# Two ranked experts of a pair, gate and up: unit by unit in turn instead of one expert after the other, with a fourth pair of half buffers

## The reference

```
vals, idx = lax.top_k(t @ router, 2)
gates     = softmax(vals)
combine   = sum(one_hot(idx, 8) * gates[..., None], 1)
for e in range(8):
    out = out + combine[:, e:e+1] * (silu(t @ wg[e]) * (t @ wu[e])) @ wd[e]
```

## Time and profile before

| | us |
|---|---|
| median of three runs | 1655.17 (1654.16 to 1659.08) |
| the profiled execution, its own time | 1653.77 |
| its span in the profile | 1652.0 |
| TensorE busy | 1599.2 (97%) |
| VectorE busy | 1216.1 (74%) |
| ScalarE busy | 980.4 (59%) |
| experts, first to last product | about 1228 to 1634 |

### The profile page before, as it was taken

One profiled execution on the slowest core, in us unless ns is written; L12 is line 12 of the kernel. 1 busy time (PEld: TensorE's weight loads), 2 busy tenths in 40 slices (PEclk: granted clock), 3 DMA queues, 4 the chain that ended last, 5 costly groups with the idle time before them and its releaser, 6 DMA issues.

```text
span 1652.0 us, 27749 instructions
## 1 busy us (share of the span) xinstructions
PE 1599.2 (97%) x10996; PEld 1449.5 (88%) x10996; DVE 1216.1 (74%) x1751; ACT 980.4 (59%) x1419; POOL 309.1 (19%) x307
## 2 busy tenths in 40 slices
PE   8999999999999999999999999999999999999997
PEld 7988888898888889998999999999997878777786
DVE  5555786666668666998875554799987887888887
ACT  6556665346657634555554443555558867777775
POOL 1331552123217501143120002132120000000000
PEclk9999999999999999999999999999999999999999
DMA  8632555555335555543435455543519999999982
GB/s 295 239 106 101 177 181 203 180 197 186 106 135 194 179 204 179 175 148 117 165 120 189 176 179 179 170 154 128 178 73 387 328 366 327 365 330 335 364 333 78
DMA packets 50774, 339.76 MB, mean 206 GB/s; under 512 B 5639, under 2 KB 7903, under 8 KB 11439
## 3 DMA queue, kind: packets, MB, share of 16 engines
q1 hardware_dynamic: 47920, 328.79, 55.9%
q0 software_dynamic: 2720, 9.13, 1.8%
HBM read 336.76 MB, written 1.13 MB: 205 GB/s over the span
## 4 chain that ended last, share of the span: by engine, by line
PE 81%; ACT 7%; DVE 6%; issue 3%; POOL 1%; DMA 0%; DVEq 0%; ACTq 0%; SPq 0%; POOLq 0%
PE bank L578 12%; PE bank L552 8%; PE bank L554 8%; PE bank L553 8%; PE bank L576 7%; ACT wh L1342 5%; PE bank L997 3%; PE bank L709 3%; PE bank L999 3%; DVE wl L1911 3%; PE bank L998 3%; PE bank L711 3%; PE bank L710 3%; PE bank L1005 1%; PE bank L1006 1%
## 5 line engine op out<-in xcount | busy, mean ns | idle before, releaser
L1911 DVE TENSOR_TENSOR wl<-stg,wh 128x2048 fp32r<-128x2048 f32 x266 | 610.8, 2304 | 209.6 <-ACT wh L1342 209.2
L1342 ACT ACTIVATE wh<-stg 128x2048 fp32r<-128x2048 f32 x266 | 507.1, 1910 | 131.0 <-PE bank L999 44.3
L552 PE MATMUL bank<-xx,wh 128*128 128x272 f32 (+1 forms) x778 | 225.5, 290 | 0.0
L554 PE MATMUL bank<-xx,wl 128*128 128x272 f32 (+1 forms) x778 | 223.3, 287 | 0.0
L553 PE MATMUL bank<-xx,wh 128*128 128x272 f32 (+1 forms) x778 | 223.1, 287 | 0.0
L578 PE MATMUL bank<-xx,wh 128*128 128x512 f32 x448 | 159.7, 396 | 0.0
L578 PE MATMUL bank<-H,wh 128*128 128x512 f32 x434 | 151.3, 390 | 0.0
L553 PEld LDWEIGHTS bank<-xx,wh 128*128 128x128 f32 x778 | 147.5, 190 | 0.0
L552 PEld LDWEIGHTS bank<-xx,wh 128*128 128x128 f32 x778 | 146.3, 188 | 1.1 <-issue 0.7
L554 PEld LDWEIGHTS bank<-xx,wl 128*128 128x128 f32 x778 | 146.3, 188 | 0.0
L709 PE MATMUL bank<-wh,xx 128*128 128x256 f32 x480 | 139.7, 291 | 0.8 <-DVE zm L1985 0.8
(11 more groups left out here) (432 smaller groups left out, 3810.7 us busy)
## 6 DMA issues: line engine op xcount, KB each, us to landing
stg<-in_w SPq DMA_DIRECT2D x178, 1024.0 KB, 5.0
stg<-in_units SPq DMA_DIRECT2D x86, 1024.0 KB, 6.9
sq<-in_units SPq DMA_DIRECT2D x22, 1024.0 KB, 6.8
stg_more<-in_units SPq DMA_DIRECT2D x20, 1024.0 KB, 6.9
BT<-bias_scratch POOLq DMA_DIRECT2D x3, 1024.0 KB, 10.5
BT<-bias_scratch POOLq DMA_DIRECT2D x1, 2048.0 KB, 12.9
BB<-bias_scratch POOLq DMA_DIRECT2D x2, 1024.0 KB, 6.5
stg<-in_tails SPq DMA_DIRECT2D x4, 512.0 KB, 4.9
```

The costliest lines, as they stand in the source:

```text
L552: pe.matmul(out, wh, xh(kt), start=kt == 0, stop=False)
L554: ins = pe.matmul(out, wl, xh(kt), start=False, stop=kt == KT - 1)
L1342: act.activation(WH[u % NW][:, :], stg[stage_of(u)][:, :], ACT.Copy).then_inc(*m.inc("w_high", u))
L1911: vec.tensor_tensor(WL[u % NW][:, :], stg[stage_of(u)][:, :], WH[u % NW][:, :].bitcast(F32), ALU.subtract).then_inc(*m.inc("w_low_v", u))
```

## The change

It takes the gate and up products of a pair's two experts unit by unit in turn, and the units are loaded in that order (`PAIR_UNITS`, `phases`): in a group first all gate rows (a unit of the big expert, one of the small, a unit of the big, one of the small), then all up rows likewise. Only the very first group (pair 0, group 0) keeps the old order. `turn` of a group moves behind the first three big gate rows of the next group, for the last group behind the first two rows of the down products; `turn_and_sum` stands three small rows further on. There is a fourth pair of half buffers (`wh_more`, `wl_more`): ScalarE may round unit u when unit u-4 is finished. Room comes from the second `G` and from one staging buffer (five instead of six). With one `G`, the gathering of the next pair's tokens stands inside the down products. The arm for the case that an expert has more than 128 tokens is changed in the same way and does not run with these inputs.

```
-MORE = 2
+MORE = 1
...
-PAIR_UNITS = [(s, 4 * gi + n) for gi in range(2) for s in range(2) for n in range(4)] + [(s, 8 + n) for s in range(2) for n in range(3)] \
-    + [(s, 11 + n) for n in range(5) for s in range(2)] + [None]
+LATER_UNITS = [(s, n) for n in range(16) for s in range(2)] + [None]
+PAIR_UNITS = [[(s, n) for s in range(2) for n in range(4)] + LATER_UNITS[8:]] + [LATER_UNITS] * 3
...
+def ring_of(u):
+    if u < RING_FROM:
+        return u % NW
+    k = (u - RING_FROM) % (NW + 1)
+    return NW if k == 0 else (RING_FROM + k - 1) % NW
+
+def last_in_ring(u):
+    return u - NW if u < RING_FROM else u - NW - 1
...
+def phases(j, gi):
+    n0, nn = GU[gi]
+    every = [(s, up, kt) for s in range(2) for up in range(2) for kt in range(KD)]
+    if j == 0 and gi == 0:
+        return [every[KD * i:KD * (i + 1)] for i in range(4)]
+    by_unit = lambda r: ((2 * KD * n0 + (r[1] * KD + r[2]) * nn) // UT, r[0], r[2])
+    return [sorted([r for r in every if r[1] == up], key=by_unit) for up in range(2)]
...
-            stg += [flat(SQ)[:, 0:UT * P], sb("stg_more", [P, UT * P], F32, st)[:, :]]
+            stg += [flat(SQ)[:, 0:UT * P]]
+            WH += [sb("wh_more", [P, UT * P], F32R, st)]
+            WL += [sb("wl_more", [P, UT * P], F32R, st)]
...
-                G = [sb(f"G{i}", [P, KD, 3 * P], F32R, sp) for i in range(2)]
+                G = sb("G", [P, KD, 3 * P], F32R, sp)
...
                     for gi in range(3):
...
+                        for i, phase in enumerate(phases(j, gi)):
+                            for s, up, kt in phase:
+                                one_row(s, gi, up, kt)
+                                if gi > 0 and (s, up, kt) == (0, 0, 2):
+                                    turn("sp", big, gi - 1, 0, mtm2[0])
+                                if gi > 0 and (s, up, kt) == (1, 0, 2):
+                                    turn_and_sum(few_, gi - 1)
+                            if gi == 0 and i == 0:
+                                if j == 0:
+                                    gather_small()
+                                else:
+                                    scatter(j - 1, (2, 3))
+                            if gi == 1 and i == 0:
+                                select(big)
+                                select(few_)
...
                     def hook(n, s, i_step):
                         if (n, s, i_step) == (0, 0, 1):
+                            turn("sp", big, 2, 0, mtm2[0])
+                        if (n, s, i_step) == (0, 1, 1):
                             turn_and_sum(few_, 2)
+                        if 0 < n < 5 and (s, i_step) == (0, 3) and j < PAIRS - 1:
+                            gather(j + 1, n - 1)
...
 class Splits
             def enter(self, u):
-                while self.made < min(u + NW, N_UNITS) and not self.held:
+                while self.made < N_UNITS and last_in_ring(self.made) < u and not self.held:
                     self.split(self.made)
                     self.made += 1
...
 ScalarE, split
-                    w.wait_ge(*m.of("group" if u - NW < EXPERT_UNIT else arm[0], ("unit", u - NW)))
-                act.activation(WH[u % NW][:, :], stg[stage_of(u)][:, :], ACT.Copy).then_inc(*m.inc("w_high", u))
+                    w.wait_ge(*m.of("group" if last_in_ring(u) < EXPERT_UNIT else arm[0], ("unit", last_in_ring(u))))
+                act.activation(WH[ring_of(u)][:, :], stg[stage_of(u)][:, :], ACT.Copy).then_inc(*m.inc("w_high", u))
...
 VectorE, sparse
+                        for i, phase in enumerate(phases(j, gi)):
+                            for s, up, kt in phase:
+                                sp.row(j, gi, s, up, kt)
+                                if gi > 0 and (s, up, kt) == (1, 0, 0):
+                                    low(big, gi - 1)
+                                if gi > 0 and (s, up, kt) == (0, 0, 6):
+                                    small_hidden(few_, gi - 1)
+                                if gi > 0 and (s, up, kt) == (1, 0, 7):
+                                    small_low(few_, gi - 1)
+                            if (0, 1, KD - 1) in phase:
+                                hidden_of("sp", big, gi, 0, mtmp[0], mtm2[0], last)
+                            if gi == 0 and i == 0:
+                                if j < PAIRS - 1:
+                                    choose(2 * j + 2)
+                                    choose(2 * j + 3)
+                                if j > 0:
+                                    scatter(j - 1, (2, 3))
```

More of the change, by code:

```diff
@@ L1007, in in_two @@
                 return product
[L1009 to L1032, removed]
@@ L1034, in turn, with row @@
-            def turn(tag, x, gi, i, j):
+            def row(tag, j, s, gi, up, kt, products, read, operand):
+                x, (n0, nn) = 2 * j + s, GU[gi]
+                first = 2 * KD * n0 + (up * KD + kt) * nn
+                if kt == 0:
+                    for i in range(len(products)):
+                        b, old = bank((tag, "gu", x, gi, up, i), (read, (x, gi, i)))
+                        held.add(b)
+                        vacant(old)
+                operand(kt)
+                pieces = [(unit_of(j, s, n), k, c, o) for n, k, c, o in pieces_of(first, nn)]
+                for i, product in enumerate(products):
+                    b = m.bank[tag, "gu", x, gi, up, i]
+                    for pi, (u, k, c, o) in enumerate(pieces):
+                        if k == 0:
+                            unit_ready(u)
+                        ins = product(PS[b][:, o * P:(o + c) * P], kt, WH[ring_of(u)][:, k * P:(k + c) * P], WL[ring_of(u)][:, k * P:(k + c) * P])
+                        over = i == len(products) - 1 and k + c == UT
+                        if kt == KD - 1 and pi == len(pieces) - 1:
+                            ins.then_inc(*m.inc(f"group_{tag}", ("gu", x, gi, up, i)))
+                            if over:
+                                m.also(f"group_{tag}", ("unit", u))
+                            let_go(b)
+                        elif over:
+                            ins.then_inc(*m.inc(f"group_{tag}", ("unit", u)))
+                at[0] += nn
@@ L1036, in turn @@
+            def turn(tag, x, gi, i, hidden):
                 nn = GU[gi][1]
@@ L1161, in nothing @@
                         pass
-                    for gi in range(3):
[L1164 to L1185, removed]
@@ L1206, in hidden_product, with turn_all @@
                     return in_three(lambda kt: EHH[s][:, kt, i * P:(i + 1) * P], lambda kt: EHL[s][:, kt, i * P:(i + 1) * P], 10)
[L1208 to L1212, removed]
+                def turn_all(j, gi):
+                    for s in range(2):
                         for i in range(2):
-                            turn("et", x, gi, i, i)
+                            turn("et", 2 * j + s, gi, i, mtm4[2 * s + i])
                 for j in range(PAIRS):
                     for gi in range(3):
[L1218 to L1223, removed]
+                        for i, phase in enumerate(phases(j, gi)):
+                            for s, up, kt in phase:
+                                row("et", j, s, gi, up, kt, [product(0), product(1)], "hidden_et" if up else "gate_et", operand)
+                            if gi > 0 and i == 0:
+                                turn_all(j, gi - 1)
+                    turn_all(j, 2)
                     down("et", j, [[hidden_product(s, i) for i in range(2)] for s in range(2)], lambda x, g, i: [("summed", (x, g, i))],
@@ L1313, in take, with row @@
                 self.at += n
+            def row(self, j, gi, s, up, kt):
+                n0, nn = GU[gi]
+                self.low = max(self.low, unit_of(j, 0, 0))
+                for n, k, c, o in pieces_of(2 * KD * n0 + (up * KD + kt) * nn, nn):
+                    u = unit_of(j, s, n)
+                    self.used[u] = self.used.get(u, 0) + c
+                while self.used.get(self.low) == UT:
+                    self.low += 1
+                self.at += nn
+                self.enter(self.low)
             def run(self, n):
```

229 lines of the change are left out of this document (110 added, 119 removed).

## The result

The changed kernel takes 1697.29 us in the median of four runs (1696.83 to 1699.4), the one before 1655.41 (four runs): a ratio of 1.0252 (95% interval 1.0233 to 1.0270). It is slower by 42 us, where 38 were forecast, and 1697 lies in the range. (A slip ahead of the prediction: the first piece of TensorE's order shown there reads G1, which is the buffer of the second and the fourth pair, so it isn't of the third.)

The account below looks back on a forecast made before the run. TensorE was taken to bound the kernel, a pair being its work plus stalls. Net stalls of +23.3 us and a slower clock of +15.2 made +38.5 on the profiled 1653.8, said as 1693 for the median; range 1670 to 1710.

Parts of the forecast that it names:

- What bounds the stage: Expert stage: a pair's 100.4 us are TensorE's work plus stalls, some 6.5 us of them; weights wait for VectorE.
- the third rival: Weight loading: with five staging buffers instead of six the weights become the bound, 1709 us; chance 0.07.
- The new stalls: At `turn`: it waits for hidden values that stand behind four splits, 48.4 us in 11 stalls.
- What it removes: In the expert stage: 16.8 us of stalls at `turn` and 9.1 us of other stalls go.
- A pair: Expert stage of the changed kernel: a pair takes 108 to 111 us instead of 100.4.
- The clock: TensorE behind the 11 new stalls: one slow stretch of 1.6 us each, less 2.4 for those of now, +15.2 us.
- The first rival: TensorE: the stalls come as worked out but the clock stays as it is, +23.3 us, 1678; chance 0.27.
- the second rival: End of a group: hidden values come in time; `turn` at E + 4.4 breaks even, at E + 2 gives 1629; chance 0.05.

Follow-up runs that it names:

- e7: The changed kernel with big hidden values ahead of both last splits, group 2's small ones ahead of a split, and later transposes at the down products: 1625.65 us, ratio 0.9816.
- e1: The changed kernel with the big expert's hidden values moved on VectorE ahead of both of the group's last splits: 1632.49 us, ratio 0.9842.
- e5: The changed kernel with the transposes of big hidden values moved from behind the third to behind the sixth big gate row of the next group: 1675.06 us, ratio 1.0101.
- e8: The changed kernel with the big expert's hidden values on VectorE between the group's last two splits: 1657.12 us, ratio 1.0013.
- e6: The changed kernel with matmuls of constants (7 and 11) ahead of the 11 late transposes, filling most of each stall: 1678.09 us, ratio 1.0141.
- e3: The changed kernel with the units and rows of gate and up in the old order again, all else as changed: 1633.63 us, ratio 0.9838.
- e4: The kernel before, with the big expert's hidden values on VectorE ahead of the split that its last up row releases: 1648.36 us, ratio 0.9954.

## Why the prediction was right, point by point

**What bounds the stage.** Right: a pair is TensorE's work plus stalls. e7 without stalls runs at 93 us for a pair (92.9 to 93.3 from one start of the down products to the next), and 100.4 less 6.5, 93.9, was said. The transfers, at 345 GB/s before, carry 374 there: they were not the bound, and the third rival is out (ScalarE waited 4 us for them in the whole stage of the changed kernel). They are near it in e7, busy 97% in the window above, and ScalarE waits 6.9 us for them.

**The new stalls.** 48.4 us forecast, 48.1 measured, in 11 cases as said, and shown by e1, e5 and e8 from both sides. The sum is better than its terms, and in that it was lucky (second pair, E is the end of the group):

| | `turn` starts, forecast | measured | stall, forecast | measured |
|---|---|---|---|---|
| group 0 | E + 6.5 (5.7 in the last pair) | E + 5.5 | 4.4 (3.6) | 3.4 |
| group 1 | E + 5.7 | E + 5.6 | 4.1 | 4.0 |
| group 2 | E + 6.3 | E + 7.9 | 4.9 | 5.5, and 0.9 ahead of the down products |

In group 0 I had VectorE too late. It was through with the choice of tokens and the additions when the up phase's first unit was ready:

```profile
1354.67 1.28 DVE L2604 TENSOR_TENSOR res<-res,bank 128x512 f32<-128x512 f32 x2
1355.86 6.82 DVE L1957 TENSOR_TENSOR wl<-stg,wh 128x2048 fp32r<-128x2048 f32 x3
```

So it began the four splits some 5.1 us into the phase, where 5.0 was reckoned for group 1. The last pair, which chooses nothing, has the same stall of 3.4. In group 2 I had it too early. The step that failed is the start of its four splits at 3.7 us into the phase; they began at 5.8. ScalarE stood still just before; the timeline of the second pair:

```profile
1406.64 0.41 DVE L2622 TENSOR_TENSOR xc<-xc,bank 128x256 f32<-128x256 f32 x1
1407.09 0.42 ACT L1805 ACTIVATE SHB<-xc 128x256 fp32r<-128x256 f32 x1 [2.69 <-DVE xc L2622]
1408.15 1.92 ACT L1390 ACTIVATE wh<-stg 128x2048 fp32r<-128x2048 f32 x1
1410.10 2.29 DVE L1957 TENSOR_TENSOR wl<-stg,wh 128x2048 fp32r<-128x2048 f32 x1 [2.14 <-ACT wh L1390]
```

ScalarE waits 2.69 us for the small expert's hidden values, which VectorE makes behind a split. The operation that waited and two more small ones (L1759, L1790) stand ahead of the split that VectorE then waits for. I had followed VectorE's queue and taken ScalarE's as free.

**What it removes.** The waits for rows are gone. The waits for half buffers in the down products went too, but one came in their place at the start, 0.9 us in each pair. I had taken all 9.1 us as gone, since with four half buffers the next down unit is split one unit earlier, and put 0.8 in the first pair; 5.0 us of such waits are there (3.7 and 1.3). This is the term that makes the stalls' net +27.2 instead of +23.3. The first down unit's split stands behind the same late splits. The timeline at that place, where the last matmul of the group had started at 1411.41:

```profile
1412.54 0.47 PE L1028 MATMUL bank<-wh,SHH 128*128 128x512 f32 x1 [0.79 <-DVE wl L1957]
```

That this wait and the longer stall have one cause was tried in e7: with the small hidden values ahead of the split both waits are gone, but e7 also moves `turn`, so for the stall at `turn` alone the two edits aren't told apart.

**A pair.** I had said 108 to 111 us as a sign; 112.7 were measured. The terms give more than the sign: 100.4 less 6.5, with 13.4 of stalls and three times 1.6 for the clock, is 112.1. And between E and `turn` in the earlier trace rows TensorE had 4.6 us of matmuls (to 1372.56), not 4.4; nothing hangs on that.

**The clock.** +15.2 forecast, 15.8 left over in the trace, 18 by e6 against the changed kernel. Eight slow matmuls for each stall were a fair mean and not what happened: the last section counts from five to nine. The first rival (stalls yes, clock no, 1678) is what e6 shows with the clock held: 1678. Here the clock fell behind all 11 stalls of 3.4 to 5.5 us, and in e5 behind three of four gaps of 2.4. The Trainium skill (TensorE: Matmul & The Clock Gate, part 1) has the clock fall only after a window without work; the gaps of 2.4 in e5 had matmuls on both sides, and the measurement decides. The same page (under "HAM oscillation") warns that a wait which comes back pays the fall each time. In the changed kernel that held 11 times of 11; in e8 one of four gaps of 3.5 us went without.

**Faster, the second rival.** The place that I named (ready at E + 4.4 or sooner breaks even) is where e8 lies: there `turn` starts at E + 4.2 on average of the 11 (cover plus stall: 3.3, 3.4 and 5.6 in the three groups), and the time equals that of before within 0.3%.

## What to carry to other kernels

Where engines run written-out orders, look what stands **ahead** of a small operation that another engine waits for: a bulk operation there that is released by the waiting engine's own progress puts its whole length, and that of its chain, into every round. What the waiting engine has to do in the meantime is the other side: here the stall was the chain less that, and it could be cured from either (e1 by a shorter chain, e3 by 7.5 us of work ahead; both with the fourth pair of half buffers, 26 and 27 us under the kernel before). With three pairs the shorter chain won 7 us, since the next unit hung on the same late split. Follow the queue of every engine in the chain: what went wrong in group 2 was one taken as free. Count what the clock takes behind a stall as a term of its own: here it was some 18 us beside 48 us of stalls.

## What the runs showed of the hardware that I had not expected

The shortest stalls were followed by the longest slow stretch. Behind the 3.65 us gap at 1361.89 nine starts in a row lie 0.43 us apart or more, and the small expert's sums behind them are slow too; behind the 5.75 us gap at 1413.77 only five are. The third pair repeats this, and in the last one the 5.75 us gap has nine as well. So the length of a stall doesn't give what the clock takes behind it. And it can fall with hardly a gap ahead: in e3, e4 and e8 it is at half in two stretches that begin at 1229 to 1232 and at 1239 to 1242, at the first expert products, with no gap over 1.1 us in the 30 us in front; this came in some runs and not in others, and why stays open. In e3 it also fell behind a gap of 1.44 us at 1301.02, and in e4 behind gaps of 1.45 and 1.91 at 1251.94 and 1253.77, while in e8 it didn't behind gaps of 2.38 and 3.54. So no length of gap parts here those that are followed by the slow clock from those that aren't. A matmul of float32 constants, 256 wide, takes 0.43 us in the fills of e6 and shows as two records 0.22 us apart, so a filler must be counted from its records and not from its width.
